# A three-layer fp32 block on one core: the first two weight chunks in quarters, small loads moved between queues, a softplus chain moved later

## The reference

```python
xn = rmsnorm(h, norm_mix_g)
u = xn @ w_in                                  # 1024 x 7168
q, k, v, xr, gr, ga, gb = split(u)             # 1024 columns each
ya = chunked_band_attention(q, k, v, rel_table) @ w_attn_out   # table bias
xc = causal_depthwise_conv(xr, conv_w, conv_b)                 # 4 taps
# rg_lru(xc): 16 blocks of 64 x 64
r, i = sigmoid(xc @ w_r + b_r), sigmoid(xc @ w_i + b_i)
log_a = -8 * r * softplus(-lam)
h_t = exp(log_a) * h_(t-1) + sqrt(-expm1(2 * log_a)) * i * xc
yb = (h_t * gelu(gr)) @ w_rnn_out
h = h + (sigmoid(ga) * ya + sigmoid(gb) * yb) @ w_o
h = h + (silu(g) * up) @ w_ffn_out             # gated MLP
# then a gated delta-rule layer and an attention layer, each with an MLP,
# and a last rmsnorm
```

## Time and profile before

| | |
|---|---|
| median of three timed executions | 1207.03 us |
| the profiled execution | 1205.23 us, span 1203.5 us |
| granted TensorE clock, mean | 0.976 |
| PE busy | 1149.0 us (95%) |
| DVE, ACT, POOL busy | 752.5, 564.8, 219.4 us |
| chain that ended last | PE 85%, DVE 9% |

### The profile page before, as it was taken

One profiled execution on the slowest core, in us unless ns is written; L12 is line 12 of the kernel. 1 busy time (PEld: TensorE's weight loads), 2 busy tenths in 40 slices (PEclk: granted clock), 3 DMA queues, 4 the chain that ended last, 5 costly groups with the idle time before them and its releaser, 6 DMA issues.

```text
span 1203.5 us, 21847 instructions
## 1 busy us (share of the span) xinstructions
PE 1149.0 (95%) x8900; PEld 1111.0 (92%) x8900; DVE 752.5 (63%) x913; ACT 564.8 (47%) x721; POOL 219.4 (18%) x226
## 2 busy tenths in 40 slices
PE   4999899999999999999999999999989999999997
PEld 4999889999999999998999998889989999888996
DVE  3755875666566553579968577764466657776433
ACT  4546456535444343456645355543344445554331
POOL 4894001402000000236372020000030002000001
PEclk9999899999999999889989899999989999999999
DMA  9744443654555555335420155555535545555531
GB/s 268 237 150 141 141 141 106 210 175 150 166 184 190 185 175 174 106 122 185 131 89 2 36 161 189 177 186 192 178 106 177 172 132 183 177 187 190 182 139 36
DMA packets 154852, 187.34 MB, mean 156 GB/s; under 512 B 6400, under 2 KB 143776, under 8 KB 154784
## 3 DMA queue, kind: packets, MB, share of 16 engines
q1 hardware_dynamic: 149072, 183.51, 46.9%
q10 hardware_dynamic: 5712, 2.86, 0.9%
HBM read 185.29 MB, written 1.07 MB: 155 GB/s over the span
## 4 chain that ended last, share of the span: by engine, by line
PE 85%; DVE 9%; issue 2%; ACT 2%; DMA 1%; POOL 1%; SPq 0%; DVEq 0%; POOLq 0%; ACTq 0%
PE PS L332 20%; PE PS L334 19%; PE PS L333 19%; PE PS L383 10%; PE PS L385 5%; DVE WL L328 2%; DVE XHL L480 1%; PE PS L392 1%; PE PS L391 1%; PE PS L390 1%; ACT WH L319 1%; PE PS L1793 1%; PE PS L1779 1%; DMA RAW<-in_w_in 1%; PE PS L672 1%
## 5 line engine op out<-in xcount | busy, mean ns | idle before, releaser
L328 DVE TENSOR_TENSOR WL<-RAW,WH 128x2048 fp32r<-128x2048 f32 x173 | 409.0, 2365 | 252.4 <-ACT WH L319 252.4
L319 ACT ACTIVATE WH<-RAW 128x2048 fp32r<-128x2048 f32 x173 | 330.0, 1910 | 248.4 <-PE PS L334 200.8
L332 PE MATMUL PS<-XHL,WH 128*128 128x256 f32 x1184 | 348.9, 295 | 27.6 <-DVE WL L328 17.2
L333 PE MATMUL PS<-XHL,WH 128*128 128x256 f32 x1184 | 342.8, 290 | 0.0
L334 PE MATMUL PS<-XHL,WL 128*128 128x256 f32 x1184 | 342.7, 289 | 0.0
L332 PEld LDWEIGHTS PS<-XHL,WH 128*128 128x128 f32 x1184 | 235.6, 199 | 33.1 <-DVE WL L328 16.9
L333 PEld LDWEIGHTS PS<-XHL,WH 128*128 128x128 f32 x1184 | 235.7, 199 | 0.3
L334 PEld LDWEIGHTS PS<-XHL,WL 128*128 128x128 f32 x1184 | 235.1, 199 | 0.0
L332 PE MATMUL PS<-HH,WH 128*128 (+1 forms) x688 | 195.0, 283 | 4.3 <-DVE SG L1576 2.8
L333 PE MATMUL PS<-HL,WH 128*128 (+1 forms) x688 | 194.7, 283 | 0.0
L334 PE MATMUL PS<-HH,WL 128*128 (+1 forms) x688 | 194.7, 283 | 0.0
(11 more groups left out here) (287 smaller groups left out, 1537.8 us busy)
## 6 DMA issues: line engine op xcount, KB each, us to landing
RAW<-in_mlp_w_up SPq DMA_DIRECT2D x32, 1024.0 KB, 5.4
RAW<-in_mlp_w_down SPq DMA_DIRECT2D x32, 1024.0 KB, 4.9
RAW<-in_w_in SPq DMA_DIRECT2D x28, 1024.0 KB, 5.1
RAW<-in_w_ffn_in_pairs SPq DMA_DIRECT2D x22, 1024.0 KB, 5.1
RAW<-in_dn_w_in SPq DMA_DIRECT2D x16, 1024.0 KB, 5.7
RAW<-in_mb_w_in SPq DMA_DIRECT2D x12, 1024.0 KB, 5.2
RAW<-in_w_ffn_out SPq DMA_DIRECT2D x11, 1024.0 KB, 5.0
RAW<-in_w_attn_out SPq DMA_DIRECT2D x4, 1024.0 KB, 5.2
```

What stands on the lines that cost most here:

```text
L319: act.activation(WH[:, k], RAW[:, k], ACT.Copy).then_inc(hi_done, 1)
L328: dve.tensor_tensor(WL[:, k], RAW[:, k], WH[:, k].bitcast(F32), ALU.subtract).then_inc(lo_done, 1)
L332: pe.matmul(out, wh, xh, start=start, stop=False, skip_group_check=True)
L333: pe.matmul(out, wh, xl, start=False, stop=False, skip_group_check=True)
```

## The change

1. SP fetches c0 and c1 in four pieces each, a piece being two row blocks (256 KB), c0's between the four parts of x. ACT and DVE split them piece by piece, with the matching pair of x. PE multiplies a piece (both column halves, 12 matmuls) as soon as it is there.
2. AROW, DTB, WBA and BIAS are issued by ACT in the turn of c6. The bias rows and WRI go to SP's queue, behind c2 and ahead of c3.
3. The squares are added by DVE, not POOL, after c1's pieces. The sums move to point 3 and the rows to point 4; `norm_root` and `norm_scale` move from the turn of c0 to that of c1.
4. The softplus chain moves from the turn of c1 to that of c4; its first two instructions and its Exp are at the very start, and an Exp of no use loads the table there. ACT waits for the chain before the first `gate_pair`.
5. On POOL the preparation of WBA moves behind the convolution.

```diff
+        def fetch_piece(eng, c, p):
+            dst = RAW[piece_of(c, p)].rearrange("p (k n) -> p k n", k=2)
+            eng.dma_start(dst, source("xr", c)[:, 2 * p:2 * p + 2, :]).then_inc(piece_landed(c, p), 16)
+        def split_hi_piece(act, c, p):
+            act.wait_ge(piece_landed(c, p), 16)
+            act.activation(WH[piece_of(c, p)], RAW[piece_of(c, p)], ACT.Copy).then_inc(s_.hi_piece if p < 3 else hi_done, 1)
+        def multiply_pieces(pe, st):
...
+            for p in range(4):
+                if c == 0:
+                    pe.wait_ge(s_.xl_ready, p + 1)
+                if p < 3:
+                    pe.wait_ge(s_.lo_piece, 3 * c + p + 1)
+                else:
+                    pe.wait_ge(lo_done, c + 1)
+                for b in range(2):
+                    for k in (2 * p, 2 * p + 1):
+                        mm = product(...)
-        SUMS_AT = [2, 1, 1, 2, 2, 2]
-        ROWS_AT = [3, 2, 2, 5, 3, 5]
+        SUMS_AT = [3, 1, 1, 2, 2, 2]
+        ROWS_AT = [4, 2, 2, 5, 3, 5]
@@ block.sync
             for p in range(4):
                 sp.dma_start(H[:, 2 * p:2 * p + 2], ...)
-            for name, n in SEGMENTS:
-                steps(sp, seg[name], lambda st: fetch(sp, st), head=SLOTS if name == "xr" else 0)
+                fetch_piece(sp, 0, p)
+            for p in range(4):
+                fetch_piece(sp, 1, p)
+            fetch(sp, Step(seg["xr"], 2, None))
+            sp.wait_ge(s_.ext_ready, 1)
+            sp.dma_start(ext_dram, EXT[:]).then_inc(s_.ext_out, 16)
...
+                    sp.dma_start(WRI[64 * e:64 * e + 64, r, :, 64 * e:64 * e + 64],
+                                 a[w].rearrange("(j e) d f -> e d j f", e=2)[e]).then_inc(s_.wri_in, 16)
+            fetch(sp, Step(seg["xr"], 3, None))
@@ block.scalar
+            act.activation(SUM[:, 0:1], EPSC[:], ACT.Exp)
             for p in range(4):
                 norm_high(act, 0, p, squares=False)
-            split_hi(act, first, 0)
+                split_hi_piece(act, 0, p)
+            squares(act, 0, 0)
+            squares(act, 0, 1)
+            act.wait_ge(s_.ey_done, 1)
+            act.activation(SMALL[:, 1, 0:8], SMALL[:, 1, 0:8], ACT.Exp, scale=-1.0).then_inc(s_.sm_ready, 1)
             for p in range(4):
-                squares(act, 0, p)
-            split_hi(act, first, 1)
+                split_hi_piece(act, 1, p)
+            squares(act, 0, 2)
+            squares(act, 0, 3)
...
             for st in (Step(seg["xr"], j, None) for j in range(4)):
                 split_hi(act, st)
-                if st.j == 0:
-                    act.wait_ge(s_.const, 1)
+                if st.j == 1:
                     norm_root(act, 0)
...
             for st in (Step(seg["qk"], j, None) for j in range(8)):
                 split_hi(act, st)
+                if st.j == 2:
+                    late_inputs()
+                if st.j == 0:
+                    act.wait_ge(s_.sp_ready, 1)
                 gate_pair(st.j)
@@ block.vector
             for p in range(4):
                 norm_low(dve, 0, p)
-            split_lo(dve, first, 0)
-            split_lo(dve, first, 1)
+                split_lo_piece(dve, 0, p)
+            for p in range(4):
+                split_lo_piece(dve, 1, p)
+            dve.wait_ge(s_.sq_done, 4)
+            ch(dve.tensor_tensor(XN[:, 0:4], XN[:, 0:4], XN[:, 4:8], ALU.add))
...
             for st in (Step(seg["xr"], j, None) for j in range(4)):
                 split_lo(dve, st)
                 if st.j == 0:
+                    continue
+                if st.j == 1:
                     norm_scale(dve, ch, 0)
                     dve.wait_ge(s_.wri_zero, 1)
+                    read_out(Step(seg["xr"], 0, None), XR[:, 0:2, 3:TOK + 3])
                 read_out(st, XR[:, 2 * st.j:2 * st.j + 2, 3:TOK + 3])
@@ block.tensor
             for st in (Step(seg["xr"], j, None) for j in range(4)):
-                times_x(0)(st)
+                if st.j < 2:
+                    multiply_pieces(pe, st)
+                    norm_point(pe, 0, 2 * st.j + 1)
+                else:
+                    times_x(0)(st)
```

More of the change, by code:

```diff
@@ L247, in build @@
         x_in = [sem(f"x_in{p}") for p in range(4)]
+        piece_in = [sem(f"piece_in{p}") for p in range(6)]
         hi_done = sem("hi_done")
@@ L260, in build @@
           amf_out yf_out ty_out zg_done vn0 vn0_out s_done s_out w_done w_out vn1 vn1_out o_done o_out osq osum osd
-          orows gated uq_zero yy oo low_out""".split()
+          orows gated uq_zero yy oo low_out hi_piece lo_piece sp_ready""".split()
         s = {n: sem(n) for n in names}
@@ L804, in _ @@
                         pool.wait_ge(s_.conv_done, j + 1)
+            pool.wait_ge(s_.row_in, 48)
+            fg, g3 = vec_at["final_norm_g"], vec_at["mix_norm_g_2"]
+            pc(pool.memset(W2[:, :, 0:1], 1.0))
+            pc(pool.tensor_tensor(W2[:, :, 1], VEC[:, fg:fg + KB], VEC[:, fg:fg + KB], ALU.mult))
+            pc(pool.tensor_tensor(G23[:], VEC[:, fg:fg + KB], VEC[:, g3:g3 + KB], ALU.mult))
+            pc.wait(pool)
+            pool.tensor_tensor(WBA[:], WBA[:], G23[:, :, None].to_broadcast([P, KB, 16]), ALU.mult).then_inc(s_.prep, 1)
+            pool.wait_ge(s_.prep, 1)
             pool.wait_ge(s_.bias_in, 16)
@@ L937, in _, with late_inputs @@
             act.dma_start(EXT[:, 127:384], a["rel_reversed"]).then_inc(s_.tab_in, 16)
-            act.dma_start(AROW[:], a["dn_a_log"].partition_broadcast(P)).then_inc(s_.row_in, 16)
-            act.dma_start(DTB[:], a["dn_dt_bias"].partition_broadcast(P)).then_inc(s_.row_in, 16)
-            act.dma_start(WBA[:], cols(a["dn_w_in"], 4096, 16)).then_inc(s_.row_in, 16)
+            act.wait_ge(s_.const, 1)
+            act.activation(SUM[:, 0:1], EPSC[:], ACT.Exp)
             act.wait_ge(s_.vec_in, 16)
-            first = Step(seg["xr"], 0, None)
             for p in range(4):
                 norm_high(act, 0, p, squares=False)
-            split_hi(act, first, 0)
-            for p in range(4):
-                squares(act, 0, p)
-            split_hi(act, first, 1)
[L949 to L959, removed]
+                split_hi_piece(act, 0, p)
[3 more added lines that the diff above has]
+            act.activation(SMALL[:, 1, 0:8], SMALL[:, 1, 0:8], ACT.Exp, scale=-1.0).then_inc(s_.sm_ready, 1)
+            for p in range(4):
+                split_hi_piece(act, 1, p)
+            squares(act, 0, 2)
+            squares(act, 0, 3)
+            def late_inputs():
+                act.dma_start(AROW[:], a["dn_a_log"].partition_broadcast(P)).then_inc(s_.row_in, 16)
+                act.dma_start(DTB[:], a["dn_dt_bias"].partition_broadcast(P)).then_inc(s_.row_in, 16)
+                act.dma_start(WBA[:], cols(a["dn_w_in"], 4096, 16)).then_inc(s_.row_in, 16)
+                act.wait_ge(s_.ext_out, 16)
+                act.dma_start(BIAS[:], bass.AP(tensor=ext_dram.tensor, offset=0, ap=[[1, P], [384, 16], [1, TOK]])).then_inc(s_.bias_in, 16)
             def sigmoid(out, ps, bias):
@@ L1221, in _, with softplus_start @@
             ch = Chain(s_.dve)
+            def softplus_start(n):
+                v = [SMALL[:, i, 0:n] for i in range(2)]
+                ch.wait(dve)
+                dve.scalar_tensor_tensor(out=v[1], in0=v[0], scalar=-1.0, in1=v[0], op0=ALU.mult, op1=ALU.max).then_inc(s_.ey_done, 1)
             def softplus(n, ready):
                 v = [SMALL[:, i, 0:n] for i in range(6)]
-                ch.wait(dve)
-                dve.scalar_tensor_tensor(out=v[1], in0=v[0], scalar=-1.0, in1=v[0], op0=ALU.mult, op1=ALU.max).then_inc(s_.ey_done, 1)
                 dve.wait_ge(s_.sm_ready, ready)
```

56 lines of the change are left out of this document (37 added, 19 removed).

## The result

Four executions of the changed kernel took 1197.61 to 1200.69 us, median 1199.03, against 1206.85 for the kernel before beside them: ratio 0.9933, 95% interval [0.9917, 0.9948]. It is faster by 7.8 us, where 5.4 were forecast. The median stands at the lower edge of the forecast's range (1198.9 to 1204.0), where rival (a) had it. The profiled execution took 1200.05 us (span 1198.3).

The account below looks back on a forecast made before the run. PE, busy 95% of the span, was taken as the bound. Starting c4 6.9 us sooner, less 1.5 for the clock, gains 5.4: 1207.03 − 5.4 = 1201.6 us, range 1198.9 to 1204.0.

Parts of the forecast that it names:

- rival (a): In c2, the clock stays up, or c3 lands sooner and the stop is shorter: 6.9 to 8.2 us gained; chance 0.26.
- Where the gain is decided and what sets it: PE's start of c4, set by c3's landing, split, root and reciprocal: 36.9 instead of 43.78, 6.9 us gained.
- The transfers: Early weight queue: c0 lands at 11.8, c2 at 17.8, c3 at 23.6 instead of 24.5, so c3 hardly comes earlier.
- the hole of 5:7: Weight queue at 5 to 7 us moved 0.24 MB where 0.7 fit; if small loads caused it, c3 lands 1.3 us sooner.
- The clock: PE's 3.1 us stop in the middle of c2 makes the granted clock fall, losing 1.5 us.
- The quarters: c0 and c1 in pieces at the start: c0 ends by 15.7, 8 us sooner, not expected to show at the end.
- rival (b): WRI, ahead of c3 in the queue, holds c3 back by 1.8 us, clock down: 3.6 us gained; chance 0.16.
- rival (d): Slower: five DMAs between c2 and c3 delay SP's issue of c3, up to 2.7 us slower, 1209.7; chance 0.05.
- Softplus, late loads, the three adds: Edits on DVE and ACT around the early chunks, expected to delay nothing PE wants; counted at nothing.
- rival (c): POOL's convolution becomes what PE waits for at its last block: only 1.7 us gained, 1205.3; chance 0.04.
- To the end: After c4 everything is paced by PE, so the 5.4 us gain carries to the end of the kernel.
- (e): The quarters' 8 us are waited off in c2, hole at c4 unchanged: at most 1 to 2 us gained; chance 0.05.

Follow-up runs that it names:

- the whole chunks: Changed kernel with c0 and c1 fetched, split and multiplied whole instead of in quarters; median 1202.46 us, ratio 0.9966 to the kernel before.
- two of the kernels above: Changed kernel with the norm's root ahead of c3's split (1196.84 us); the same with c3 also fetched ahead of bias rows and WRI (1197.75 us).

## Why the prediction was wrong, step by step

- **Where the gain is decided and what sets it**: right. c3's landing, its split, table, root and reciprocal are the chain; from landing to rows the prediction had 4.5 us and the trace has 4.37. The stop stood where it was said, released by the reciprocal.
- **The transfers**: the step that failed. The prediction charged the small loads with their share of the engines' time, 0.8 us, and kept the hole of 5:7 as a bound ("If the small loads caused that hole too, c3 lands 1.3 us sooner, 22.3"). They did cause it: late alone, they gave c0 1.85 us, and early again they took 2.4 from c2. Over 3 to 13 us 2.5 us of bytes were missing before, and c2 came 2.6 sooner than before, not 1.4. c3 landed at 22.2, the bound. WRI and the bias rows cost 2.6 us between c2 and c3 (22.20 − 16.60 − 3.0), for the 2.8 taken from the row. The estimate from the Trainium skill (DMA: Bandwidth & Descriptors, Why small descriptors are slow), 27% of overhead for a 256-byte descriptor, was 1.8 for WRI (redone with 0.52 MB, 1.5 us without overhead, it is 1.9); the measurement decides, and stands by the row.
- **The clock**: a consequence. The stop was 1.85 us, not 3.1, and the clock stayed at 1.00. The term fits a stop of the forecast length (2.97 us: 1.5 lost), with the reserve that another stop of 0.96 stood before that one. Here the two errors have one sign: 1.4 us from c3, 1.5 from the clock, and 0.1 from the steps behind; 5.4 + 3.0 = 8.4, what the gates show. The far end of rival (a), 8.2, is this sum. The forecast itself, added up term by term, hid that the first term decides whether the second exists: 1.3 us of transfer were worth 2.8.
- **The quarters**: right in size (first matmul 7.21, c0 done 15.5). The prediction did not expect to see their 8 us at the end; the whole chunks show that 5.1 of 7.7 us reach the gates, with the changed queues as they are.
- **WRI's price, rival (b)**: it did not come true. The prediction's 25.4 and 22.6 for the end of WRI are 2.8 us apart and do not give its 1.8.
- **SP's issues, rival (d)**: it did not come true. Five DMAs were issued in 7 us, and 1.9 us more of delay changed nothing.
- **Softplus, late loads, the three adds**: at nothing, right. The chain ended at 45.2, its gates followed at once, and the late loads went out at 49.5 to 51.5. The hole before c4 is gone, and would be 0.56 us if the chain had stayed.
- **The convolution, rival (c)**: 2.9 us to spare predicted for a gain of 5.4, 3.0 measured with 8.4. It started at 28.3, 1.0 sooner than the prediction had it, and one instruction fewer met a split (9 for 10), 1.9 us, which the 2.9 did not count: 5.6 + 3.9 + 1.9 − 8.4 = 3.0. It is the next bound, and was reached in two of the kernels above.
- **To the end**: 8.4 us at the gates came out as 5.2 and 6.5 in the two profiled executions, and by the ratios as 8.1 and 10.5 us in the two sets of timed ones (by the medians 7.8 and 9.0). What the runs showed of this is that the clock's falls behind the norms differ between executions of one program, and that stretches at a granted clock of 1.00 differ too, by 1.5 us; whether the earlier start shifts them in one direction on average stays open.
- **The chances**: (c) and (e) alone are 0.09, more than the 0.07 given to "same", so the 0.89 for "faster" is at least 0.02 too high.

## What to carry to other kernels

A hole in a saturated transfer stream with a few tiny loads beside it is worth taking as theirs: price it by the bytes that are missing over the whole stretch in which they run (0.9 MB, 2.5 us here), not by the share of time that the tiny loads take (0.8 us). When one term of a sum decides whether another exists, as the length of a stop decides whether the clock falls, compute the whole sum for each end of the uncertain term, since both errors then go the same way. And once a stop at the start is gone, ask which queue order made it: moving the one chunk that PE needs next ahead of the small weights brought the gates another 2.3 us forward.

## What the runs showed of the hardware

- 431 packets of 0.02 MB in all, in the second queue, took 13.1% of the engines' time in 5:7 and left the first queue 60.5% in place of 103.6%, 0.41 MB in place of 0.65. The two add up to 73.6%: a part of the time the engines were idle.
- c3's issue, held for 1.94 us (14.83 to 16.77), left its landing where it was (22.20 and 22.28), as long as the queue had WRI to move. Held for 3.1 us more, it landed 3.0 later.
- PE's clock kept its level over stops of 1.46, 1.85, 1.93 and 2.41 us in the middle of c2 and fell behind stops of 2.97 (with one of 0.96 before it) and 4.22, each time for 1.5 us of lost time.
- One program, two traces: 147 and 159 matmuls in the same 20 us of a PE that never waits, at a granted clock of 0.83 and 0.90.
- At the start a matmul takes 0.21 us, and 0.12 from 20.5 us in the kernel before; the column of the granted clock shows 1.00 there all the same (15 to 25 us). The pace is to be read from the matmuls.
- The same 80 us of work took 80.46 us before, and 81.94 and 80.50 in the changed kernel's two traces, at a granted clock of 1.00 and the same waits.
